# Second block of a two-block layer stack: gates projected with the values, context loaded transposed, rows spread by transfers, first eight positions from 8x8 sums, last four rows in halves

## The reference

```python
sh1, sc1, g1, sh2, sc2, g2 = _adaln(c, w_ada, b_ada)            # modulation of the latents
csh1, csc1, ... = _adaln(c_ctx[None], w_ada, b_ada)             # and of the context
h_lat = _rms(x, g) * (1 + sc1) + sh1
h_ctx = _rms(ctx, g) * (1 + csc1) + csh1                        # 256 context tokens
pl = _split_in(h_lat @ w_in); pc = _split_in(h_ctx @ w_in)
# parts: mLSTM q, k, v, o, 16 mLSTM gates, attention q, k, v, branch gates
m_lat = mlstm(...)     # 4 heads of 128, forward and backward over context, then latents
a_lat = window_attention(...)   # 8 query heads, 2 kv heads, context keys, a sink
y = (sigmoid(g_m) * (m_lat @ w_bm) + sigmoid(g_a) * (a_lat @ w_ba)) @ w_out
x = x + g1 * y
x = x + g2 * _peer(_rms(x, g') * (1 + sc2) + sh2, w_query, sub_keys, u, v)
```

```python
q = (x @ w_query).reshape(tokens, 8, 2, 128)
s = einsum('mhpd,hpnd->mhpn', q, sub_keys)        # two lists of 128 scores
s1, i1 = top_k(s[:, :, 0], 16); s2, i2 = top_k(s[:, :, 1], 16)
cand = s1[..., :, None] + s2[..., None, :]        # 16 x 16 sums
top, pos = top_k(cand, 16); idx = i1 * 128 + i2 at pos
act = gelu(einsum('mhkd,md->mhk', expert_u[idx], x))
return einsum('mhk,mhkd->md', softmax(top) * act, expert_v[idx])
```

## Time and profile before

| | us |
|---|---|
| median of three runs (1325.68 to 1327.37) | 1326.92 |
| the profiled execution | 1327.63 |
| its span, first to last instruction | 1325.8 |
| TensorE busy | 1181.1 (89%) |
| VectorE busy | 865.2 (65%) |
| ScalarE busy | 318.1 (24%) |
| GpSimd busy | 330.3 (25%) |
| moved by the DMA queues | 386.91 MB |

### The profile page before, as it was taken

One profiled execution on the slowest core, in us unless ns is written; L12 is line 12 of the kernel. 1 busy time (PEld: TensorE's weight loads), 2 busy tenths in 40 slices (PEclk: granted clock), 3 DMA queues, 4 the chain that ended last, 5 costly groups with the idle time before them and its releaser, 6 DMA issues.

```text
span 1325.8 us, 14774 instructions
## 1 busy us (share of the span) xinstructions
PE 1181.1 (89%) x5152; PEld 710.4 (54%) x5152; DVE 865.2 (65%) x2315; ACT 318.1 (24%) x1024; POOL 330.3 (25%) x278
## 2 busy tenths in 40 slices
PE   8999999989999999998999889889877777777776
PEld 5876667857856768764566444445322223233332
DVE  2746745365542678675487677777777777777655
ACT  0114400243210233231132222222222122222212
POOL 0000000000000000000055454445755454454430
PEclk9999899999999999999999999999999999999999
DMA  8761145731344445543399999999999999999994
GB/s 341 291 248 65 64 190 202 291 114 65 127 191 159 144 181 191 200 167 110 127 386 425 424 424 425 423 425 423 423 424 422 423 424 422 423 422 423 424 423 196
DMA packets 50330, 386.91 MB, mean 292 GB/s; under 512 B 5712, under 2 KB 8400, under 8 KB 10832
## 3 DMA queue, kind: packets, MB, share of 16 engines
q0 software_dynamic: 36864, 268.45, 48.5%
q1 hardware_dynamic: 13392, 117.51, 23.7%
HBM read 384.89 MB, written 1.05 MB: 291 GB/s over the span
## 4 chain that ended last, share of the span: by engine, by line
PE 56%; DMA 33%; DVE 5%; ACT 3%; issue 2%; POOL 1%; SPq 0%; DVEq 0%; ACTq 0%; POOLq 0%
PE bank L523 23%; PE bank L529 14%; DMA const<-peer_uv_in,arena 11%; DMA wring<-peer_uv_in,arena 10%; PE bank L1124 8%; DMA arena<-peer_uv_in,arena 7%; DMA hT<-peer_uv_in,arena 5%; PE bank L564 2%; PE bank L754 1%; PE bank L597 1%; PE bank L667 1%; PE bank L726 1%; DVE arena L1585 1%; PE bank L928 1%; PE bank L1006 1%
## 5 line engine op out<-in xcount | busy, mean ns | idle before, releaser
L1124 PE MATMUL bank<-arena 128*128 128x512 f32 x460 | 221.5, 618 | 47.9 <-ACT arena L1553 47.3
L1124 PE MATMUL bank<-wring,arena 128*128 128x512 f32 x340 | 165.9, 624 | 36.8 <-ACT arena L1553 36.2
L523 PE MATMUL bank<-wring,hT 128*128 128x256 f32 (+2 forms) x640 | 187.9, 451 | 2.6 <-ACT hT L1214 1.7
L529 PE MATMUL bank<-hT,wring 128*128 128x256 f32 (+1 forms) x1088 | 188.6, 333 | 0.5 <-ACT hT L1225 0.4
L529 PEld LDWEIGHTS bank<-hT,wring 128*128 128x128 f32 x1088 | 169.0, 192 | 26.0 <-issue 11.5
L2265 DVE CUSTOM_DVE_ANT_0 arena<-arena 128x1024 f32<-128x1024 f32 x115 | 140.6, 1224 | 58.3 <-DMA arena<-peer_uv_in,arena 56.7
L2360 POOL DMA_INDIRECT arena<-peer_uv_in,arena x115 | 137.9, 1200 | 160.3 <-PE bank L1124 125.1
L1124 PEld LDWEIGHTS bank<-arena 128*128 128x128 f32 x460 | 85.6, 195 | 167.2 <-issue 91.6
L2333 POOL TENSOR_TENSOR small<-small,const 128x1 f32<-128x1 f32 (+3 forms) x18 | 16.2, 898 | 625.7 <-DVEq L1597 284.5
L523 PEld LDWEIGHTS bank<-wring,hT 128*128 128x128 f32 x640 | 120.3, 191 | 62.6 <-issue 48.1
L2265 DVE CUSTOM_DVE_ANT_0 wring<-wring,arena 128x1024 f32<-128x1024 f32 x85 | 103.9, 1223 | 45.2 <-DMA wring<-peer_uv_in,arena 45.2
(11 more groups left out here) (210 smaller groups left out, 1278.7 us busy)
## 6 DMA issues: line engine op xcount, KB each, us to landing
wring<-w_in SPq DMA_DIRECT2D x22, 2048.0 KB, 8.4
wring<-ada_in SPq DMA_DIRECT2D x12, 2048.0 KB, 8.3
wring<-wo_in SPq DMA_DIRECT2D x5, 2048.0 KB, 8.1
...
```

What stands on the lines that cost most here:

```text
L523: ins = pe.matmul(bank[:, 0:cols], lhs[k], w[:, k, 0:cols], start=(k == 0), stop=(k == n - 1))
L529: ins = pe.matmul(bank[:, at:at + n_tok], w[:, k, col:col + P], rhs[:, k, :], start=(k == 0), stop=(k == KC - 1))
L1124: ins = pe.matmul(sums_of[half][:, :], diag[:, at % NDIAG, :], v_row[slot_of[at]][:, half * 512:(half + 1) * 512], start=(n == 0), stop=(n ...
```

## The change

Seven edits, all in the second block:

1. **Context columns.** The context is also loaded transposed (`ctxT`, by GpSimd's queue). The inverse roots go to memory (`ctx_scratch`) and come back on all partitions (`ctx_root`); VectorE multiplies `hT` by them, ScalarE applies the modulation in eight operations. Transposes "hc" go.
2. **Gate columns.** The weights of (w2, 0, 2) get 16 more columns, the mLSTM gates; `values_and_gates(tt)` projects 272 columns where the 16 were projected, and the later "akv" products go. The weights no longer take a ring slot but a place of their own, loaded before (wo, 1, 0).
3. **Rows spread by transfers.** SyncE writes the two gate vectors and the eight key rows to memory (`scratch`) and loads them back broadcast. `gb`, `g_diag`, `key_rows` go. All this stands behind the load of (w2, 0, 6).
4. **Orders in the projections.** Query norms and keys go ahead of the gates' chain on VectorE; `mlstm_queries(0)` behind `attn_scores(1)`.
5. **Merge and first queries.** The last merge copy goes to ScalarE; head 0's first query half waits per column block; both output products of tile 1 stand ahead of head 1's queries.
6. **First eight positions.** `first_eight()` takes the top 8 of each score list and the top 8 of the 8x8 sums, decodes and hands them to GpSimd before the full 16x16 choice.
7. **Last four rows.** Rows 252 to 255 are gathered in halves, the four u halves first, then the four v halves; TensorE waits for the v half.

```diff
-        chunks += [("w2", 0, 5), ("ada", 0, 6), ("w2", 0, 0), ("w2", 0, 2), ("ada", 0, 7), ("w2", 0, 1), ("w2", 0, 3)]
+        chunks += [("w2", 0, 5), ("ada", 0, 6), ("w2", 0, 0), ("ada", 0, 7), ("w2", 0, 1), ("w2", 0, 3)]
+        IN_GATED, GATED = NW + 2, 256 + 16
+        place[("w2", 0, 2)] = (IN_GATED, 0)
+        loads.insert(loads.index(("wo", 1, 0)), ("w2", 0, 2))
...
+            def values_and_gates(tt):
+
+                w = weights(("w2", 0, 2)).rearrange("p (k c) -> p k c", k=KC)
+                project(("akv", tt), [hT[:, k, tt * P:(tt + 1) * P] for k in range(KC)], w, GATED)
...
-                context(8 + t)
+                values_and_gates(t)
...
-            for tt in range(2, 4):
-                project(("wg", tt), [hT[:, k, tt * P:(tt + 1) * P] for k in range(KC)], wg2, 16)
+            values_and_gates(2)
+            values_and_gates(3)
...
-            for tt in range(4):
-                project(("akv", tt), [hT[:, k, tt * P:(tt + 1) * P] for k in range(KC)], w, 256)
-            w_used(("w2", 0, 2), ("akv", 3))
...
-            context(10)
-            context(11)
...
-            head_queries(1)
+            rows_back(0)
             for half in range(2):
                 taken(pe, ("gT", 1, half))
             out_rows(0, 1)
+            out_rows(1, 1)
+            head_queries(1)
             head_scores(1)
-            out_rows(1, 1)
...
+                    if at >= APART:
+                        pe.wait_ge(sem(f"values_full{slot_of[at]}"), 16 * values_nth(at))
...
+                if chunk == ("w2", 0, 6):
+
+                    for n, (m, adds) in enumerate(((2, 2), (5, 3))):
+                        sp.wait_ge(sem("ada_bias"), adds)
+                        sp.dma_start(scratch[n:n + 1, :].rearrange("o (k p) -> p (o k)", p=P), modT[:, m, :, 0],
+                                     allow_slow_non_contiguous=True).then_inc(sem("gate_out"), 16)
+                    sp.wait_ge(sem("gate_rows"), 1)
+                    full(sp, ("fc",))
+                    for d in range(2):
+                        sp.dma_start(scratch[2 + 2 * d:4 + 2 * d, :].rearrange("a (b c) -> (a b) c", b=2),
+                                     rows[5 + d][4 * d:4 * d + 4, :]).then_inc(sem("keys_out"), 16)
+                    sp.wait_ge(sem("gate_out"), 32)
+                    for n in range(2):
+                        sp.dma_start(gate_rows[n], scratch[n:n + 1, :].to_broadcast([P, D])).then_inc(sem("gates_in"), 16)
+                    sp.wait_ge(sem("keys_out"), 32)
+                    for h in range(MH):
+                        for d in range(2):
+                            row = scratch[2 + 2 * d + h // 2:3 + 2 * d + h // 2, (h % 2) * 512:(h % 2 + 1) * 512]
+                            sp.dma_start(spread_rows[2 * h + d], row.to_broadcast([P, 512])).then_inc(sem(f"key_rows{h}"), 16)
...
-                    act.wait_ge(sem("mix_gain"), 1)
-                    for t in range(TT):
-                        modulated("hc", t, 0, 0, 1, 0)
+                    act.wait_ge(sem("ctx_scaled"), 1)
+                    for k in range(KC):
+                        ins = act.activation(hT[:, k, 0:S], hT[:, k, 0:S], ACT.Identity, scale=modT[:, 1, k, 1:2],
+                                             bias=modT[:, 0, k, 1:2])
+                    ins.then_inc(sem("ctx_columns"), 1)
...
-                    for t in range(TT):
-                        modulated("hc", t, 1, 0, 1, 0)
+                    dve.wait_ge(sem("in_ctxT"), 16)
+                    dve.wait_ge(sem("ctx_root"), 16)
+                    link(tt(hT[:, :, 0:S], hT[:, :, 0:S], every(ctx_root, KC), ALU.mult), "ctx_scaled")
...
+                dve.wait_ge(sem(f"key_rows{h}"), 32)
                 for d in range(2):
-                    bank = full(dve, ("G", d, h))
...
+            def first_eight():
+
+                n = TOPK // 2
+                first, second = score[:, 0, 0, :], score[:, 0, 1, :]
+                a8, b8 = slice(0, n), slice(TOPK, TOPK + n)
+                sums = cand[:, 0:n * n]
+                pair_of = lambda buf: buf.rearrange("p (a k) -> p a k", a=2)[:, :, 0:n]
+                dve.wait_ge(sem("scores"), 1)
+                step(dve.max(tops[:, a8], first))
+                step(dve.max(tops[:, b8], second))
+                settle()
+                step(tt(sums.rearrange("p (a b) -> p a b", a=n), every(tops[:, a8], n, 2), every(tops[:, b8], n), ALU.add))
+                step(dve.max_index(topi[:, a8], tops[:, a8], first))
+                step(dve.max_index(topi[:, b8], tops[:, b8], second))
+                settle()
+                step(dve.max(best[:, 0:n], sums))
...
+                step(dve.max_index(bpos[:, 0:n], best[:, 0:n], sums))
+                decode(0, "idx_first", n)
+                step(dve.match_replace(work_a, tops[:, a8], first, -3e38))
+                step(dve.match_replace(work_b, tops[:, b8], second, -3e38))
...
+                    if at < APART:
+                        pool.indirect_dma_start(out=pair[here], out_offset=None, in_=a["peer_uv"],
...
+                    pool.indirect_dma_start(out=u_row[here], out_offset=None, in_=a["peer_uv"],
...
+                    for n in ([at - LEAD] if at < ROWS - 1 else range(at - LEAD, ROWS)):
+                        if n >= APART:
+                            s = n % (2 * TOPK)
+                            pool.indirect_dma_start(out=v_row[slot_of[n]], out_offset=None, in_=a["peer_uv"],
```

272 lines of the change are left out of this document (132 added, 140 removed).

## The result

| | before | changed |
|---|---|---|
| median, first chip | 1326.98 | 1307.92 (1304.14 to 1310.54, 4 runs) |
| ratio, first chip | | 0.9859 (0.9840 to 0.9878) |
| median, the same kernel on a second chip | 1326.15 (1323.71 to 1329.52, 11 runs) | 1306.76 (1304.07 to 1307.48, 5 runs) |
| ratio, second chip | | 0.9847 (0.9833 to 0.9861) |
| profiled execution, first chip | 1327.63 | 1304.14 |

The profiled execution is 23.5 us faster, the medians 19.1 and 19.4. I first go through the profiled one stage by stage, then come to the difference. Single runs of one kernel lie up to 6 us apart, those of the kernel before too.

A forecast was written before the change was run, and what follows sets the result against it. TensorE's order was taken to bound the kernel up to about 650 us, the gather's transfers from 662 on. Terms -0.7, -14.5, -5.5, -2.6 and -1.0 sum to -24.3: 1327.6 to 1303.3, median frame 1302.6, stated 1303; range 1296 to 1313.

The forecast's parts named there:

- Projections: 385 to 491 us: narrow gate matmuls, spreading matmuls, slow stretches and short waits leave TensorE's path; -14.5 us in sum.
- two slow stretches: Projections, 32 instructions at 389.09 and 64 at 424.70: expected to run at full clock, gaining 1.7 and 1.4 us.
- short waits for ScalarE: Behind the projections: TensorE waits less for ScalarE's copies, as it has fewer to make; about 0.7 us gained.
- the clock's part: Projections: 3.1 us gained if TensorE's clock no longer falls once narrow matmuls are gone; called not safe.
- mLSTM: 554 to 605 us: eight key-row matmuls leave TensorE (6.9 us), VectorE takes part back; -5.5 us, ends -2 and -6.9.
- SyncE's block: SyncE's queue before ada chunk 9: writes, landings and ten broadcasts end at 486 to 488 us; cost 0.
- rival D: SyncE's block makes it slower, 1328 to 1334 us: four-byte elements hold an engine 0.309 us each, stores 39.5 us; chance 0.05.
- Layer 1: Context columns: 16 transposes and copies replaced by a multiply and eight affine operations; -0.7 us, between 2 gained and 1 lost.
- I take 2.9, as the fixed part of so short an operation is most of it: Layer 1, context columns: ScalarE's eight affine operations, put between 2.9 and 5.9 us, were taken at 2.9.
- Gather start: First gather 7.6 us earlier within its stage, but the tenth waits for row 0; -2.6 us, ends 0 and -7.6.
- gain 684.9 - 683.1 = 1.8, or 3.3 by the larger slack: Gather start: queue runs dry for 5.7 us until the tenth gather near 683.1, before the change 684.9 at the earliest.
- Tail: Last four rows gathered in halves, TensorE ending 3.2 us behind the last landing, was 4.6; -1.0 us, ends 0 and -2.5.

The follow-up runs named there:

- experiment 1: The changed kernel run again with no edit, on the second chip; median 1306.76 us (1304.07 to 1307.48).
- experiment 5: Changed kernel with the 16 gate columns multiplied in narrow runs of their own in their old places, wide products later; 1318.23 us (1311.58 to 1320.51).
- Experiment 6: Changed kernel with key rows spread again by eight TensorE matmuls, SyncE writing and spreading only the gate vectors; 1314.58 us (1311.96 to 1316.38).
- experiment 10: Changed kernel with SyncE writing eight more vectors of 1024 four-byte elements behind the gates' chain and waiting for them; 1343.82 us (1340.86 to 1346.09).
- experiment 7: Changed kernel with the first eight positions chosen from the full 16x16 sums again; 1306.16 us, ratio 0.9855 (0.9839 to 0.9872).
- experiment 3: Changed kernel with the last four rows gathered whole again; 1306.81 us (1305.76 to 1310.16).

## Why the prediction was right, point by point

| stage, between two points of TensorE or the span | forecast | first trace | the other trace |
|---|---|---|---|
| layers, up to 283.05 (no edit) | 0 | -1.95 | -1.05 |
| layer 1 to the transposes of 385.45 | -0.7 | +0.7 | +2.3 |
| projections, to 489.65 | -14.5 | -14.2 | -14.2 |
| attention and mLSTM, to 604.43 | -5.5 | -6.4 | -6.4 |
| merge, to 644.71 | 0 | 0 | 0 |
| gather, to the dot product of row 224 | -2.6 | -0.6 | -0.1 |
| tail | -1.0 | -1.1 | -1.1 |
| sum | -24.3 | -23.5 | -20.5 |

(Points are given by their start in the kernel before; the other trace is experiment 1's. Without the first row, which no edit touches on TensorE, the change gained 21.5 and 19.4 us of the 24.3 forecast.)

- **Projections.** Right in size, and in its two large parts: the gate columns gained 7.3 and the spreading matmuls 3.4, as said. The two slow stretches gave 3.4 for 3.1, and the 0.7 for short waits for ScalarE didn't come (the 0.84 us ahead of 458.41 stand there as they did ahead of 479.01). The reason of the clock's part is only half shown: a fall behind 32 narrow instructions came back with them (experiment 5), the one at 389 did not. By the rule of the Trainium skill (TensorE: Matmul & The Clock Gate, Part 4: PE-mode transpose) the transposes that remain could have kept the stretches slow. They didn't here: behind them stand 1.00 and 13.90 us.
- **mLSTM.** The mechanism was right, the term under-sized by 0.9, by its first part. I took 1.72 us for a pair of key-row matmuls; in the kernel before it is 1.91 us from the start of a pair to the next instruction (553.92 to 555.83), 7.6 for four, and the instructions beside them start closer together without them. What VectorE took back is near what I allowed, 1.7 us of idle time (0.34 and 1.38) for 1.4. Experiment 6 puts the matmuls back: TensorE has no idle time there, and it costs the same 6.4.
- **SyncE's block.** Cost 0, as said: the ada load at 483.19, inside the 482 to 488 I gave. But rival D was nearer than I made it. In experiment 10 eight vectors in a row took 37.2 us, 4.6 for each, or an estimated 0.072 us of an engine for an element, if all sixteen share evenly; I had put a landing of 4 to 5 us against rival D's 0.309 us an element. The two vectors of the change were cheaper and lay where nothing waited for them. From 457 to 466 the engines are busy for 0.81 of the time, 7.3 us, and move 234 GB/s, or 2.1 MB. At the gather's 423 GB/s the weights' load is 5 us of that, so an estimated 2 us of all engines are left for the two vectors. In the open place behind the gates' chain the block lasted 35.8 us longer and the time grew by 36 to 37, so the slack there is a few us at most; I had counted 3 to 9. Why eight in a row cost so much more than two beside a load was not tested. The Trainium skill (DMA: Bandwidth & Descriptors, the table at its start) has the rule that transfers under 512 B don't reach the line rate; here 1 GB/s were measured against 423.
- **Layer 1.** The term had the wrong sign, +0.7 for -0.7. The step that failed is "I take 2.9, as the fixed part of so short an operation is most of it": the eight affine operations take 4.04 us for twice the columns, not 2.94. All traces of the changed kernel and its variants also show a fall of the granted clock between 285 and 300 (0.89 to 0.97), which the one trace of before doesn't have there. The hole of 2.34 us doesn't cause it in the first trace, where the fall stands ahead of the hole: 16 instructions at 288.38 take 5.38 us, in experiment 1 3.69, and the hole swallows the difference. In experiment 1 it stands behind the hole of 4.03 (four instructions at 296.99 take 1.09 for 0.60) and costs the 1.6 us that this trace has more. What brings it was not shown.
- **Gather start.** The mechanism held: first gather 28.8 us earlier (28.3 said), tenth 19.8 (19), a rest of the transfers before it, and in experiment 7 the first eight's shortcut is worth nothing that can be seen. That the two numbers fit so well is in part luck, as 1.95 us of both come from the first 283 us, where no edit changed TensorE's work. Within the stage, from 644.71, the first gather is 7.0 us earlier for 7.6, the tenth 2.0 later for 1.5, and the rest of the transfers is some 2.7 us (660.7 to 663.3) for 5.7. The size was off by 2.0: the step "gain 684.9 - 683.1 = 1.8, or 3.3 by the larger slack" took the queue as full again once the tenth gather was out. It isn't: the transfers move 365 and 393 GB/s from 665 to 675, where 424 is the rate of the long stretch. My reading, not tested alone, is that with the cushion gone the next gathers come at the pace at which TensorE frees slots. Also, the slots of the first nine don't come free at once: the gather at 645.26 waits 4.68 us for an output product, as the one at 672.68 did before (4.83).
- **Tail.** -1.1 for -1.0.
- **The rest.** Profiled 1304.1 for 1303.3, median 1307.9 for 1302.6. That the profiled run fits to 0.8 is luck: without the 1.95 us of the first part, which no edit touches on TensorE, it misses by 2.8. The medians' gain is 4 us less than the profiled pair's, and experiment 1 shows where they can go: the first part, the dearer fall of the clock in layer 1, and one behind TensorE's idle time of 2.6 us at row 0. The last stands in four of the eight traces that have this idle time (experiments 1, 3, 5 and 7), costs 1.7 us (5.37 for 3.67), and the forecast had it not at all: it counted that gap as covered by the transfers.
